# Gate and up weights in 16 KB runs a partition, with the features of x reordered to match

## The reference

```python
h = modulate(x, g_pre_ffn, shift, scale)              # rms_norm(x, g) * (1 + scale) + shift
logits = jnp.einsum('btd,de->bte', h, w_router)
aff = jax.nn.softmax(logits, axis=-1)
g, idx = lax.top_k(jnp.swapaxes(aff, 1, 2), cap)      # cap: 64 latent rows, 16 context rows an expert
xg = jax.vmap(lambda hb, ib: hb[ib])(h, idx)
a = jnp.einsum('becd,edf->becf', xg, w_gate)          # 16 experts, each weight 1024 x 1024 fp32
u = jnp.einsum('becd,edf->becf', xg, w_up)
y = jnp.einsum('becf,efd->becd', jax.nn.silu(a) * u, w_down) * g[..., None]
```

## Time and profile before

| what | us |
|---|---|
| runs, median (lowest to highest) | 945.46 (945.16 to 948.37) |
| the profiled execution, own time | 947.62 |
| its span, first to last instruction | 945.6 |
| TensorE busy in the span | 888.0 (94%) |
| weight loads of the experts, queue q1 | 68.0% of the 16 engines' span |

### The profile page before, as it was taken

How to read it: one execution, slowest core, us unless ns; L and a number is a source line. 1 busy time by engine, 2 the same in 40 slices (tenths; PEclk the granted TensorE clock), 3 DMA queues, 4 the chain that set the end, 5 groups by cost and what they waited for, 6 DMA issues and landing times. The chain is left out here.

```text
span 945.6 us, 19892 instructions
## 1 busy us (share of the span) xinstructions
PE 888.0 (94%) x8633; PEld 442.5 (47%) x8633; DVE 365.0 (39%) x974; ACT 216.4 (23%) x528; POOL 102.6 (11%) x137
## 2 busy tenths in 40 slices
PE   3999998899899999879999999999999999999985
PEld 3544444677655665533344443443443444433432
DVE  4256534887767765821112022021113120210136
ACT  3132213676645653410000000000000000000012
POOL 1021200000000000110110111011001101110225
PEclk9899999999999999889999999999999999999997
DMA  9997441400001119869999999999999999999984
GB/s 342 345 380 267 180 176 59 159 2 1 2 1 46 45 47 376 296 230 409 398 395 412 398 397 407 400 397 397 410 398 398 395 411 398 398 405 389 357 312 157
DMA packets 77717, 269.31 MB, mean 285 GB/s; under 512 B 6208, under 2 KB 9984, under 8 KB 77632
## 3 DMA queue, kind: packets, MB, share of 16 engines
q1 hardware_dynamic: 72384, 251.42, 68.0%
q0 software_dynamic: 4160, 13.90, 5.1%
q10 hardware_dynamic: 1088, 2.74, 0.7%
HBM read 252.06 MB, written 15.99 MB: 283 GB/s over the span
## 5 line engine op out<-in xcount | busy, mean ns | idle before, releaser
L954 PE MATMUL ps<-ring,reg 128*32 128x512 f32 x1792 | 201.6, 592 | 0.0
L1813 DVE TENSOR_SCALAR mod<-ps,kt 64x512 f32<-64x512 f32 x30 | 22.5, 749 | 254.8 <-PE ps L954 254.6
L954 PEld LDWEIGHTS ps<-ring,reg 128*32 128x32 f32 x1792 | 58.0, 110 | 113.3 <-issue 104.8
L968 PE MATMUL ps<-ring,values_in 128*32 128x256 f32 x1536 | 93.5, 386 | 2.2 <-ACT reg L1320 1.1
L1324 ACT ACTIVATE reg<-ps 128x256 f32<-128x256 f32 x16 | 6.1, 384 | 358.0 <-PE ps L1008 352.8
L954 PE MATMUL ps<-ring,kt 128*32 128x512 f32 x768 | 86.8, 592 | 0.0
L810 PE MATMUL ps<-ring,reg 128*128 128x512 f32 x160 | 76.4, 604 | 0.0
L968 PEld LDWEIGHTS ps<-ring,values_in 128*32 128x32 f32 x1536 | 50.2, 112 | 52.4 <-issue 23.9
L656 PE MATMUL ps<-ring,reg_qt 128*128 128x512 f32 x160 | 70.6, 594 | 0.0
L968 PE MATMUL ps<-ring,reg 128*32 128x256 f32 x1024 | 64.4, 395 | 1.8 <-DMA ring<-in_w_down 1.2
L1267 ACT ACTIVATE ring<-ps 128x640 f32<-128x640 f32 (+3 forms) x80 | 44.4, 555 | 72.1 <-PE ps L739 69.5
(11 more groups left out here) (238 smaller groups left out, 1000.0 us busy)
## 6 DMA issues: line engine op xcount, KB each, us to landing
ring<-in_w_up SPq DMA_DIRECT2D x32, 2048.0 KB, 21.3
ring<-in_w_down SPq DMA_DIRECT2D x32, 2048.0 KB, 21.2
ring<-in_w_gate SPq DMA_DIRECT2D x16, 2048.0 KB, 19.8
reg_qt<-in_w_gate SPq DMA_DIRECT2D x16, 2048.0 KB, 20.5
ring<-in_w_ada SPq DMA_DIRECT2D x12, 2048.0 KB, 12.6
reg<-in_x_sample SPq DMA_DIRECT2D x8, 512.0 KB, 6.3
ring<-in_w_in SPq DMA_DIRECT2D x2, 2048.0 KB, 14.0
ring<-in_w_out SPq DMA_DIRECT2D x2, 2048.0 KB, 10.1
```

Source lines behind the costliest of these rows:

```text
L954: last = pe.matmul(o[64 * n + r:64 * n + r + 32, :], x(4 * hf + j, r), w[:, j, n * HALF:(n + 1) * HALF], start=(hf == 0 and j == 0), stop= ...
L968: last = pe.matmul(o[32 * q:32 * q + 32, :], x(c), w[:, j, q * QUART:(q + 1) * QUART], start=(c == 0), stop=(c == KC - 1))
L1813: dve.tensor_scalar(put_l[:, n * HALF:(n + 1) * HALF], ps[rows, 3, :], g_l[rows, e:e + 1], None, ALU.mult)
```

## The change

Three things change together. Gate and up halves are read so that partition p takes features 4p to 4p+3 of the half: one run of 16 KB. Down halves are loaded as before. The turns of x take every fourth column of a half instead of 128 neighbouring ones (`feature_block`), so that block c holds features h*512 + 4q + j for q = 0..127. The router weights and the FFN half of the gain are loaded in that order (w_router in two loads of 256 B runs, the gain by eight loads of single elements on 32 partitions each), and the columns of shift and scale are turned by four turns to 64 partitions instead of two to 128, and copied with four copies instead of two (for the scale, a wait and two more operations apply the gain).

```diff
+
+        def feature_block(row, c):
+
+            return row.rearrange("p (h q j) -> p h j q", h=2, j=4)[:, c // 4, c % 4, :]
         def ring_slot(s):
...
-        N_CONSTS = 10
+        N_CONSTS = 19
...
             def load_consts():
-                sp.dma_start(wr[:, :].rearrange("p (c e) -> p c e", e=E),
-                             A["w_router"][0].rearrange("(c p) e -> p c e", p=P)).then_inc(consts_in, 16)
+                wr_rows = A["w_router"][0].rearrange("(h p j) e -> h p j e", h=2, j=4)
+                sp.dma_start(wr[:, 0:4 * E].rearrange("p (c e) -> p c e", e=E),
+                             wr_rows[0]).then_inc(consts_in, 16)
+                sp.dma_start(wr[:, 4 * E:].rearrange("p (c e) -> p c e", e=E), wr_rows[1]).then_inc(consts_in, 16)
+                ffn_columns = A["g_pre_columns"].rearrange("(q j) (m h b) -> b h m q j", j=4, m=2, h=2)
+                for b, h in itertools.product(range(4), range(2)):
+                    sp.dma_start(gpre[32 * b:32 * b + 32, KC + 4 * h:KC + 4 * h + 4], ffn_columns[b][h][1],
+                                 allow_slow_non_contiguous=True).then_inc(consts_in, 16)
...
             def expert_weight(e, kind, half, s):
-                src = w[0].rearrange("e (c p) n -> e p c n", p=P)[e][:, 4 * half:4 * half + 4, :]
-                sp.dma_start(ring_slot(s).rearrange("p (c n) -> p c n", c=4), src).then_inc(slot_in[s], 16)
+                if kind < 2:
+                    src = w[0].rearrange("e (h p j) n -> e h p (j n)", h=2, j=4)[e][half]
+                    sp.dma_start(ring_slot(s), src).then_inc(slot_in[s], 16)
+                else:
+                    src = w[0].rearrange("e (c p) n -> e p c n", p=P)[e][:, 4 * half:4 * half + 4, :]
+                    sp.dma_start(ring_slot(s).rearrange("p (c n) -> p c n", c=4), src).then_inc(slot_in[s], 16)
             def store_x1(o):
...
-                for j in range(2):
-                    last = pe.transpose(ps[:, 7, j * P:(j + 1) * P], modq[:, m, j * P:(j + 1) * P], ident[:, :])
+                for j in range(4):
+                    last = pe.transpose(ps[0:P // 2, 7, j * P:(j + 1) * P], modq[:, m, j:QUART:4], ident[:, :])
...
-                                        xr[:, t, (4 * half + c) * P:(4 * half + c + 1) * P], ident[:, :])
+                                        feature_block(xr[:, t, :], 4 * half + c), ident[:, :])
             def route_logits(o):
...
-                    last = pe.transpose(ps[:, 5 + c // 4, c % 4 * P:(c % 4 + 1) * P], xg_c[:, c * P:(c + 1) * P], ident[:, :])
+                    last = pe.transpose(ps[:, 5 + c // 4, c % 4 * P:(c % 4 + 1) * P], feature_block(xg_c, c), ident[:, :])
             def turn_rows_l(pair):
-                    last = pe.transpose(ps[:, 5 + c // 4, c % 4 * P:(c % 4 + 1) * P], xg_l[:, c * P:(c + 1) * P], ident[:, :])
+                    last = pe.transpose(ps[:, 5 + c // 4, c % 4 * P:(c % 4 + 1) * P], feature_block(xg_l, c), ident[:, :])
...
         def _(act):
-            act.dma_start(gpre[:, :], A["g_pre_columns"]).then_inc(early_in, 16)
+            act.dma_start(gpre[:, 0:KC], A["g_pre_columns"][:, 0:KC]).then_inc(early_in, 16)
...
-            cols = ps[:, 7, 0:2 * P].rearrange("p (j q r) -> p q j r", j=2, q=4)
+            cols = ps[0:P // 2, 7, :].rearrange("p (j h u r) -> p u h j r", j=4, h=2, u=2)
             def columns(m):
-                    dst = cmod[:, n, cond, :].rearrange("p (q j) -> p q j", j=2)
-                    if n % 2 == 0:
-                        last = dve.tensor_copy(dst, cols[:, :, :, cond])
-                    else:
-                        g = gpre[:, (n // 2) * KC:(n // 2 + 1) * KC].rearrange("p (q j) -> p q j", j=2)
-                        last = dve.scalar_tensor_tensor(dst, cols[:, :, :, cond], 1.0, g, ALU.add, ALU.mult)
+                    for u in (0, 1):
+                        part = slice(P // 2 * u, P // 2 * (u + 1))
+                        last = dve.tensor_copy(cmod[part, n, cond, :].rearrange("p (h j) -> p h j", h=2), cols[:, u, :, :, cond])
+                if n % 2:
+                    dve.wait_ge(consts_in, 16 * N_CONSTS)
+                    link(last)
+                    for cond in (0, 1):
+                        g = gpre[:, (n // 2) * KC:(n // 2 + 1) * KC]
+                        last = dve.scalar_tensor_tensor(cmod[:, n, cond, :], cmod[:, n, cond, :], 1.0, g, ALU.add, ALU.mult)
```

## The result

The changed kernel takes 987.06 us in the median of four runs (983.72 to 990.54), the kernel before 945.58 (945.16 to 948.37), also of four; the table ahead of the change has 945.46, the median of three of these. The ratio is 1.044 (95% interval 1.041 to 1.047). The profiled execution took 990.54 us with a span of 988.5, so 42.9 us more than the span before. The forecast of 944.6 and its range of 940 to 962 were both missed.

A forecast was written before the change was run, and what follows sets the result against it. TensorE's own instructions were taken to set the time, with DMA only just keeping up. 947.62 - 1.24 (weight stall) - 0.1 (gathers) + 0.44 (extra turns) gave 946.7 profiled, 944.6 as median; range 940 to 962.

The forecast's parts named there:

- no change in the landing time: Expert-stage gathers beside larger weight packets: they still land after about 8 us, so only -0.1 us.
- the first gather: First gather of latent rows, ahead of the expert stage's steady part: TensorE stands 5.50 us for it, taken as unchanged.
- Gathers come late: Rival, expert stage: each gather packet waits for a weight packet four times as long; up to +23 us, 968; chance 0.26.
- Down halves keep packets of 4 KB: Argument against late gathers in the expert stage: the down weights' loads stay in 4 KB packets; no size given.
- the stall of the earlier trace: TensorE's one stop for a weight load, at 864.08 us in the expert stage: it goes, -1.24 us.
- the small edits at the start: `mod_columns`, `columns` and constant loads: +0.44 us for extra turns, the rest covered, 3 us at most for shifted loads.
- What would show it: Signs to read in the new profile: q1's packet count, turn loads and pace, the 864 us stall, gather landings, weight waits.
- the stepped turns: Turns of x reading every fourth column: loads up to about 190 ns, hidden, cost 0; as rival +11 us, 956, chance 0.12.
- a margin of 0.4 us: Expert stage: the median gather lands in 8.0 us, 0.4 before TensorE wants its rows, 8.4 us after issue.

The follow-up runs named there:

- e3: The changed kernel with each later gather issued one expert earlier: 945.30 us, ratio 1.000 to the kernel before.
- e1: The kernel before with only the gate and up halves loaded in runs of 16 KB: 980.33 us, ratio 1.037.
- e2: The changed kernel with gate and up halves back in runs of 4 KB, turns still with a step of four: 947.63 us, ratio 1.001.
- e9: The changed kernel with later gathers one expert earlier and the two gate(1) loads held until the first gather has landed: 937.58 us, ratio 0.992.
- e12: The kernel before with only the down halves in runs of 16 KB: 955.31 us, ratio 1.010.
- e11: The changed kernel with 24 calls of unused products ahead of the wait for each of six later gathers: 986.79 us, ratio 1.044.

## Why the prediction was wrong, by its own steps

**The failed step** is "I take no change in the landing time, as all rows with a full stream give 8 us and the bytes beside it are the same". Every landing that I had was beside packets of at most 4 KB, so they could not bear on 16 KB; equal bytes per time is not equal time per turn of the queues. The landing went to 14.4 us in the median of six, and e3 shows what hangs on it: with the gathers out of the way the change takes 945.3 us. That this is 0.7 from the forecast is partly luck, since the first gather (7.4 us and not 5.5) and the turns cost what the forecast had at nothing. The rival "Gathers come late" was the right mechanism. The rule cited beside it, the Trainium skill's "DMA: Bandwidth & Descriptors", section "Queues, rings and completion order", that an engine serves its queues a whole packet at a time, agrees with the trace: 263 long packets for 254 of q0, and landings of 8.0 and 14.4 us.

**The rival was under-sized** at 968. It put 3.8 us on a gather; 6.4 was measured (8.0 to 14.4). It counted only the gather's own eight packets an engine, where 16 of q0 pass between issue and landing; 16 by its 0.48 us would be 7.7, an upper value, since more than one short packet passed each time before. It also had nothing on the clock: 1.9 us for each stop of 5 to 7 us. "Down halves keep packets of 4 KB" was true and no protection, as the gathers from the second of the six on met mostly up halves. It was right that all of TensorE's work stands behind the turns and that each microsecond past the margin counts in full.

**Right:** the stall of the earlier trace rows went; q1's packets fell by 24176 (24600 forecast, so the runs are not cut); the stream rose to 414 to 417 GB/s (408 forecast); nothing new waits in the small edits at the start. "What would show it" named the landings and the wait before the turns, and that is what it was.

**Right in kind, wrong in size:** the stepped turns. Loads rise to "about 190" by forecast, to 211 ns by measurement, the median of L837 ahead of the stage, and 209 for L947 in e3. In the changed kernel L947 reads more, since most of its loads stand behind a stop, at the granted clock of 0.50 (in e1, without the step, the median there is 225):

```profile
L947 PEld LDWEIGHTS ps<-ident,reg x64: 195/226/231, 417.3 to 868.4; 128*128 128x128 f32 x64
L947 PE MATMUL ps<-ident,reg x64: 281/417/462, 417.4 to 868.7; 128*128 128x128 f32 x64
```

They are nearly hidden: eight turns at 373.60 last until the next product at 374.56, 120 ns each, where before it was (372.55 - 371.68) / 8 = 109 ns. So 11 ns a turn, 1.4 us over the 128 and 0.4 for the extra ones in `mod_columns`; e2 measured +2.2 us in the medians, 1.3 by the ratio. The Trainium skill's penalty for a new line at each access ("Advanced Engine Details and Errata", section "SBUF Cachelines") shows in the load, 141 to 211 ns, and only about a sixth of it in the time (11 of 70 ns), since the load runs beside the product before it.

**The chance** was set too low: 0.26 on late gathers, though I had named a margin of 0.4 us, the thinnest in the profile, and had no row of the new operation.

## What to carry to other kernels

Look at who shares the DMA engines with a stream before making its packets longer: a small transfer with a thin margin pays for packets that gain the stream only 3 to 4%. Issue such a transfer early, and keep the first one free of other loads: with both (e9) the long runs bring the kernel to 0.8% under the one before, with the early gathers alone (e3) they change nothing, and with neither they cost 4.4%. Count all packets of the small transfer's queue, also those of its neighbours there. Where a row has never seen the new operation, a margin of 0.4 us is a reason for a high chance on the late case and not for zero.

## What the runs showed of the hardware

Landing of a gather of 128 rows of 4 KB, beside a full stream: 8.0 us with runs of 4 KB, 9.2 with 8 KB, 14.4 with 16 KB of the gate and up halves (medians). It follows the long packets that start before it lands: with 0 to 3 of them 7.7 to 8.9 us, with 146 or 149 it is 10.9 to 11.9, with 284 to 292 it is 14.3 to 14.8. About one passes for each packet of the gather's queue (263 for 254). A faster stream changes which load is in the air at a given moment, by one and a half to two halves here, and so the landing of a transfer that itself is unchanged. After a stop of 6.4 us on a full TensorE the granted clock is 0.50 for 5.3 us of its work; after one of 2.6 us it drops too (e12: 0.60 from 503 to 507 us), and after the stops of 0.4 to 1.5 us in e11 it does not. At 364 to 371 us the changed kernel's clock dipped once with no stop of that length, 1.6 us; in e3, the same program up to there, it is 1.00 from 362 to 371. So the dip is not part of the change, and why it comes isn't shown.
